# The later modulation sums on TensorE, behind the native tiles, in place of ScalarE and GpSimd

## The reference, cut to what matters

```python
mod = (jax.nn.silu(c) @ w_ada[i] + b_ada[i])[:, None, :]      # w_ada: 2048 x 12288
sh1, sc1, g1, sh2, sc2, g2 = jnp.split(mod, N_MOD, axis=-1)   # six vectors of 2048
hl = rmsnorm(x, norm1_w[i]) * (1.0 + sc1) + sh1
out_l, _, _ = token_mixer(hl, s_f, s_b, grid, lp)             # Hyena and SSD branches
x = x + g1 * out_l
hl2 = rmsnorm(x, norm2_w[i]) * (1.0 + sc2) + sh2
x = x + g2 * sqrelu_mlp(hl2, w_mlp1[i], w_mlp2[i])
```

## Time and profile before

| | |
|---|---|
| median of 3 executions | 4385.58 us (4385.01 to 4386.99) |
| the profiled execution | 4384.95 us |
| its span, first to last instruction | 4383.2 us |
| TensorE busy (matmuls) | 4238.8 us, 97% |
| GpSimd busy | 3536.8 us, 81% |
| VectorE busy | 2403.6 us, 55% |
| ScalarE busy | 1756.3 us, 40% |
| mean granted TensorE clock | 0.981 |

### The profile page before, as it was taken

The page is one execution under the profiler, slowest core; times in us unless marked ns, Lnnn a source line. Parts: engine busy times, 40 slices in busy tenths (PEclk is TensorE's granted clock), DMA queues, the critical chain, the costliest instruction groups (busy, mean ns, idle before and its releaser), DMA issues.

```text
span 4383.2 us, 66380 instructions
## 1 busy us (share of the span) xinstructions
PE 4238.8 (97%) x24638; PEld 3647.1 (83%) x24638; DVE 2403.6 (55%) x3732; ACT 1756.3 (40%) x1994; POOL 3536.8 (81%) x2700
## 2 busy tenths in 40 slices
PE   8999898998999999999999999999999999999998
PEld 6778676587888888888888988899888888888887
DVE  4342466534333335544322432788857957885795
ACT  4333443244444444443344434543334333333433
POOL 5755897077888888888789977987988998898897
PEclk9999898899999999999999999999999999999999
DMA  9834676044555554444455544444554454454453
GB/s 378 332 116 181 251 304 262 0 163 165 182 188 185 186 187 172 164 163 166 159 202 186 208 154 144 176 171 164 183 183 173 174 194 170 172 193 177 174 180 144
DMA packets 116320, 813.72 MB, mean 186 GB/s; under 512 B 13479, under 2 KB 17864, under 8 KB 19016
## 3 DMA queue, kind: packets, MB, share of 16 engines
q1 hardware_dynamic: 109008, 789.40, 49.0%
q10 hardware_dynamic: 7096, 21.20, 1.3%
HBM read 804.26 MB, written 6.29 MB: 185 GB/s over the span
## 4 chain that ended last, share of the span: by engine, by line
PE 62%; POOL 23%; DVE 7%; issue 6%; ACT 1%; DMA 1%; POOLq 0%; SPq 0%; DVEq 0%; ACTq 0%
PE psum L536 30%; POOL w_lo L457 19%; PE psum L540 16%; POOL ada_acc L487 4%; PE psum L525 1%; PE psum L527 1%; PE psum L526 1%; PE psum L688 1%; DVE out_hl L3098 1%; DVE out_hl L3096 1%; PE psum L1286 1%; DVE hid L3094 1%; PE psum L671 1%; PE psum L672 1%; PE psum L673 1%
## 5 line engine op out<-in xcount | busy, mean ns | idle before, releaser
L457 POOL TENSOR_TENSOR w_lo<-ring,w_hi 128x512 fp32r<-128x512 f32 x2416 | 3131.8, 1323 | 600.5 <-ACT w_hi L1362 585.4
L1362 ACT ACTIVATE w_hi<-ring 128x1024 fp32r<-128x1024 f32 x1228 | 1292.2, 1060 | 1856.3 <-PE psum L540 1641.0
L536 PE MATMUL psum<-hc_hl,w_hi 128*128 128x512 f32 x5120 | 1310.8, 398 | 25.6 <-DVE hc_hl L2006 9.7
L536 PEld LDWEIGHTS psum<-hc_hl,w_hi 128*128 128x128 f32 x5120 | 924.3, 189 | 205.5 <-issue 16.9
L540 PEld LDWEIGHTS psum<-hc_hl,w_lo 128*128 128x128 f32 x5120 | 700.2, 191 | 52.6 <-POOL w_lo L457 1.5
L540 PE MATMUL psum<-hc_hl,w_lo 128*128 128x256 f32 x5120 | 715.5, 283 | 1.1 <-POOL w_lo L457 1.1
L536 PE MATMUL psum<-out_hl,w_hi 128*128 128x512 f32 x2048 | 515.2, 393 | 4.4 <-DVE out_hl L3098 2.6
L536 PEld LDWEIGHTS psum<-out_hl,w_hi 128*128 128x128 f32 x2048 | 369.3, 189 | 71.9 <-DVE out_hl L3098 3.4
L487 POOL TENSOR_TENSOR ada_acc<-ada_acc,ada_row 128x512 f32<-128x512 f32 x224 | 288.5, 1318 | 28.6 <-ACT ada_row L1519 21.7
L540 PEld LDWEIGHTS psum<-out_hl,w_lo 128*128 128x128 f32 x2048 | 279.5, 190 | 20.0
L540 PE MATMUL psum<-out_hl,w_lo 128*128 128x256 f32 x2048 | 285.6, 282 | 0.0
(11 more groups left out here) (451 smaller groups left out, 5235.2 us busy)
## 6 DMA issues: line engine op xcount, KB each, us to landing
ring<-stream SPq DMA_DIRECT2D x620, 1024.0 KB, 4.8
ring<-mixed SPq DMA_DIRECT2D x96, 1024.0 KB, 6.4
ada_in<-ada SPq DMA_DIRECT2D x32, 1024.0 KB, 7.4
kv_dram<-kv_out ACTq DMA_DIRECT2D x32, 128.0 KB, 4.1
x<-x ACTq DMA_DIRECT2D x2, 2048.0 KB, 9.7
kv<-kv_dram ACTq DMA_DIRECT2D x2, 2048.0 KB, 9.2
mem_raw<-mem SPq DMA_DIRECT2D x2, 1024.0 KB, 6.4
ctx_raw<-ctx ACTq DMA_DIRECT2D x1, 2048.0 KB, 12.5
```

The lines of the kernel that those rows point to most:

```text
L457: m = pool.tensor_tensor(w_lo[:, slot, c:c + 4], ring[:, s, h * KC // 2 + c:h * KC // 2 + c + 4], w_hi[:, slot, c:c + 4].bitcast(F32), ALU ...
L536: pe.matmul(psum[:, b, :].rearrange("p (s t) -> p s t", s=2), w_hi[:, slot, c], x_hl[c], start=start(c), stop=False, skip_group_check=True)
L1362: act.activation(w_hi[:, 2 * (s % 2) + h], ring[:, s, k], ACT.Copy).then_inc(hi_ready, 1)
```

## The change

The 64 later tiles keep their place in the queue, two behind each native tile, but they are laid out by output columns: pair j holds 256 of the 8192 columns for all 2048 inputs. `ada_row`, `ada_acc`, their semaphores, `scale_rows`, GpSimd's loop, `ada_columns` and `ada_mod` are gone. `native(i)` now ends with `gate_rows(i)`: 16 fp32 matmuls, each with one column of `c_silu` as stationary operand and 256 moving columns, dealt over the four column groups of bank 5. ScalarE copies the bank to a free part of `xbc` (`gate_rows_out`), and behind the next native tile `gate_turn` sums the four groups and turns them into two columns of bank 2. One VectorE addition at the end of the stage adds all biases. SyncE frees the slots of these tiles by `ada_pe`. Bank 5 is new for this, so the heads write banks 4 and 6, the states 4 and 6, and the state products 6 and 4; the second state product and its masks move from head pair 3 to the start.

```diff
@@ SyncE, slot_free
-                sp.wait_ge(ada_scaled, 2 * (m // 3) + m % 3)
+                sp.wait_ge(ada_pe, ADA_1 + 2 * (m // 3) + m % 3)
@@ GpSimd
-        pool.wait_ge(half_done, 2 * FIRST["out1"])
-        for n in range(ADA_2 // KC):
-            for k in range(1, KC):
...
-                for c in range(0, D, 512):
-                    m = pool.tensor_tensor(ada_acc[:, n % 2, c:c + 512],
-                                           (ada_row[:, 0] if k == 1 else ada_acc[:, n % 2])[:, c:c + 512],
-                                           ada_row[:, k % 2, c:c + 512], ALU.add)
-                m.then_inc(ada_done, 2 if k == 1 else 1)
@@ TensorE
             m.then_inc(nat_done, 1)
+            gate_rows(i)
+
+        def gate_turn(j):
+
+            pe.wait_ge(ada_copied, ADA_G + j + 1)
+            for b in range(2):
+                m = pe.matmul(psum[:, 2, 2 * j + b:2 * j + b + 1], xbc[:, 10 + j % 2, 1, b * P:b * P + P],
+                              col("pick", 0), start=True, stop=True)
+            m.then_inc(ada_turned, 1)
+
+        def gate_rows(j):
+
+            if j:
+                gate_turn(j - 1)
+            for half in range(2):
+                m = 3 * j + 1 + half
+                w = ring[:, m % RING].rearrange("p k n -> p (k n)").rearrange("p (k n) -> p k n", n=T)
+                pe.wait_ge(mix_landed[m % RING], 16 * (m // RING + 1 + ADA_1 // 4))
+                for k in range(8):
+                    r = 32 * (k % 4)
+                    i = pe.matmul(psum[r:r + 1, 5, 0:T], c_silu[:, 8 * half + k, 0:1], w[:, k],
+                                  start=half == 0 and k < 4, stop=half == 1 and k >= 4)
+                i.then_inc(ada_pe, 1)
-        def ada_columns(n):
-
-            pe.wait_ge(ada_done, KC * (n + 1))
-            pe.wait_ge(s_mod, n + 1)
-            for k in range(KC):
-                m = pe.matmul(psum[:, 2, k:k + 1], ada_acc[:, n % 2, k * P:k * P + P], const[:, ONES, 0:1],
-                              start=True, stop=True)
-            m.then_inc(ada_sum, 1)
-                m = pe.matmul(psum[:, (2, 6)[n % 2], :], b_nat[:, g, tb], xw[:, tb, :], start=tb == 0, stop=tb == 1)
+                m = pe.matmul(psum[:, (4, 6)[n % 2], :], b_nat[:, g, tb], xw[:, tb, :], start=tb == 0, stop=tb == 1)
-            o = psum[64 * (hh % 2):64 * (hh % 2) + 64, 4 + (hh // 2) % 2, 0:T]
+            o = psum[64 * (hh % 2):64 * (hh % 2) + 64, (4, 6)[(hh // 2) % 2], 0:T]
         state_products(0)
+        state_products(1)
...
-            if p == 3:
-                pe.wait_ge(ssd_cbm, 4)
-                state_products(1)
...
-            if p in (0, 3, 6):
-                ada_columns(p // 3)
-        ada_columns(3)
+        gate_turn(NATIVE - 1)
@@ ScalarE
-                act.activation(ada_row[:, t % 2], w, ACT.Copy, scale=c_silu[:, t % KC, 0:1]).then_inc(ada_scaled, 1)
+        def gate_rows_out(j):
+
+            act.wait_ge(ada_pe, ADA_1 + 2 * j + 2)
+            if j >= 2:
+                act.wait_ge(ada_turned, ADA_G + j - 1)
+            act.activation(xbc[:, 10 + j % 2, 1], psum[:, 5, 0:T], ACT.Copy).then_inc(ada_copied, 1)
@@ VectorE
         state_masks(0)
+        state_masks(1)
...
-        ada_mod(3)
         pair_out(7)
+        dve.wait_ge(ada_turned, ADA_G + NATIVE)
+        dve.tensor_tensor(mod[:, ADA_1:, 0], psum[:, 2, 0:ADA_2], col("b_ada", ADA_1, ADA_2), ALU.add).then_inc(s_mod, 1)
@@ the layout of the weights
-    sums = ada_sums(one["w_ada"][:, ADA_1 * P:]).reshape(NATIVE, 2, P, D)
+    sums = one["w_ada"][:, ADA_1 * P:].reshape(2, 8, P, NATIVE, T).transpose(3, 0, 2, 1, 4).reshape(NATIVE, 2, P, D)
```

More of the change, by code:

```diff
@@ L172, in build @@
     kv_out = at("kv_out", [P, 3, T], 203)
-    ada_acc = at("ada_acc", [P, 2, D], 40)
-    ada_row = at("ada_row", [P, 2, D], 56)
     ctx_raw = at("ctx_raw", [P, KC, T], 176)
@@ L307, in build @@
     nat_done, z_out, hy_out = sem("native_done"), sem("z_out"), sem("hy_out")
-    ada_done, ada_sum, x_full = sem("ada_added"), sem("ada_summed"), sem("x_full")
+    x_full = sem("x_full")
     s_const, s_cols, s_c = sem("const_landed"), sem("columns_landed"), sem("c_landed")
@@ L315, in build @@
     s_csilu, s_mod, s_scales = sem("c_silu_ready"), sem("mod_ready"), sem("scales_ready")
-    ada_scaled = sem("ada_scaled")
     ada_copied, ada_turned = sem("ada_copied"), sem("ada_turned")
@@ L754, in state_products @@
             for tb in range(2):
-                m = pe.matmul(psum[:, 6, tb * T:tb * T + T], xbc[:, 8 + g, 0, tb * P:tb * P + P], xbc[:, 10 + g, 0, :],
+                m = pe.matmul(psum[:, (6, 4)[g], tb * T:tb * T + T], xbc[:, 8 + g, 0, tb * P:tb * P + P], xbc[:, 10 + g, 0, :],
                               start=True, stop=True)
@@ L1535, in _ @@
         for i in range(HEAD_SLOT):
+            if i:
+                gate_rows_out(i - 1)
             if i < ZB:
                 z_gate(i)
-            scale_rows(i)
             if i == 5:
@@ L1544, in _ @@
             slot = HEAD_SLOT + 3 * p
+            gate_rows_out(slot - 1)
             head_exps(2 * p + 1)
-            scale_rows(slot)
+            if slot + 1 < NATIVE:
+                gate_rows_out(slot)
             if p < HEADS // 2 - 1:
@@ L1549, in _ @@
             if slot + 1 < NATIVE:
-                scale_rows(slot + 1)
-                scale_rows(slot + 2)
+                gate_rows_out(slot + 1)
+        gate_rows_out(NATIVE - 1)
         act.wait_ge(hd_y, HEADS)
@@ L1638, in half_high @@
                            flat[:, 2048 + 1024 * q:3072 + 1024 * q], ACT.Copy).then_inc(gn_hi, 1)
-        act.wait_ge(ada_sum, ADA_2 // KC)
         act.wait_ge(y_y, 2)
@@ L1655, in _ @@
         split_stage("out1", RING, KC - RING)
-        act.wait_ge(s_mod, 5)
+        act.wait_ge(s_mod, 2)
         norm_act("x2", x, lambda k: mod[:, 3 * KC + k, 0:1],
@@ L2076, in pair_out @@
             dve.wait_ge(hd_y, 2 * j + 2)
-            dve.scalar_tensor_tensor(y_ssd[:, j], xbc[:, j, 0], col("ssd_d", j), psum[:, 4 + j % 2, 0:T],
+            dve.scalar_tensor_tensor(y_ssd[:, j], xbc[:, j, 0], col("ssd_d", j), psum[:, (4, 6)[j % 2], 0:T],
                                      ALU.mult, ALU.add).then_inc(hd_yc, 1)
@@ L2271, in hy_conv @@
                                      out_[:, :, 0:GRID_W - 1], ALU.mult, ALU.add).then_inc(hy_out, 1)
[L2273 to L2277, removed]
         for n in range(4):
@@ L2289, in _ @@
             dve.wait_ge(ssd_st, 2 * n + 2)
-            dve.tensor_copy(state[:, d, g], psum[:, (2, 6)[n % 2], :]).then_inc(ssd_stc, 1)
+            dve.tensor_copy(state[:, d, g], psum[:, (4, 6)[n % 2], :]).then_inc(ssd_stc, 1)
             if n >= 2:
@@ L2296, in state_masks @@
             c_ = cb[:, g]
-            p6 = psum[:, 6, :]
+            p6 = psum[:, (6, 4)[g], :]
             dve.tensor_copy(c_[:, P:T], p6[:, P:T])
@@ L2337, in _ @@
             slot = HEAD_SLOT + 3 * p - ZB
-            if p == 3:
-                state_masks(1)
             head_decay(2 * p + 1)
@@ L2345, in _ @@
                 pair_out(p - 1)
-            if p in (1, 4, 7):
-                ada_mod(p // 3)
             hy_conv(slot)
@@ L2550, in residual @@
                 add(n // RING - 1, j)
-        dve.wait_ge(s_mod, 5)
+        dve.wait_ge(s_mod, 2)
         st.did(dve.scalar_tensor_tensor(scales[:, 2], mod[:, 4 * KC:5 * KC, 0], 1.0, col("norm2", 0, KC),
@@ L3177, in ada_rows @@
     return tiles.reshape(-1, P, D)
-def ada_sums(w):
-    return w.reshape(KC, P, w.shape[1] // D, D).transpose(2, 0, 1, 3).reshape(-1, P, D)
 def packed_blocks(w, per):
```

6 lines of the change are left out of this document (removed).

## The result

The changed kernel took 4400.02 us (4398.84 to 4400.31, six executions), the kernel before 4385.54 us (4382.44 to 4387.55, six executions). The ratio is 1.0032, with a 95% interval of 1.0022 to 1.0042: the change makes the kernel slower by 14.5 us. The forecast was 4396 us in a range of 4387 to 4414, with 0.65 on slower. The profiled execution has a span of 4397.8 us, 14.6 us more than before.

What follows compares the result with a forecast made beforehand. GpSimd bounds the stage, TensorE close behind; TensorE's summed program ends the last head at 756.9 against 746.2 for no change, so +10.7 us on the median of 4385.58 gives 4396 us, range 4387 to 4414.

Steps and rivals of the forecast that it cites:

- The bound: In the stage, GpSimd bounds with TensorE close behind; TensorE has only 32.9 us idle to take the additions over.
- The sum of the stage: TensorE's program from 385.1: 284.7 us stays, 76.2 added, 6.7 wait, 3.4 half clock, 0.8 copy; last head ends 756.9.
- pair of row matmuls: Added TensorE block per two tiles: 1.94 us, a third of the way from 1.83 to 2.17; 62.1 us in all.
- state matmuls: Work that stays on TensorE: four state matmul pairs of L746 at 1.71 us each, 6.8 us.
- wait before head 0: TensorE's 10.6 us wait before the first head shrinks to 6.7 us, as GpSimd no longer slows VectorE there.
- half clock: TensorE loses 1.7 us behind L735 and once more behind the wait for head 0: 3.4 us together.
- Issue pace: Rival, chance 0.18: row matmuls go at 0.064 us an instruction, 2.17 us a pair, 7.4 us more, 4403 us.
- All waits go: Rival, chance 0.11: pairs of 1.83 us, 3 us wait for head 0, no half clock; 4386 us, nothing won or lost.
- Faster: Rival, chance 0.04: a pair costs what one L608 block costs, 0.97 us; 31 us go, 4365 us.
- The clock: Rival, chance 0.04: one-column row matmuls leave TensorE at half clock, up to 1.7 us a tile; 4420 us if a fourth do.
- The queue: SyncE's ring loads: a native's tile lands in about 8 us, needed 9.4 us after its request; covered by 1 us.
- The end of the stage: After the last head the filter's loads are exposed (four issues, some 2 us landing); L814 starts about 6.4 us later.

Runs made afterwards that it cites:

- the half rows: The changed kernel with 8 of the 16 row matmuls of each pair left out, all loads kept: 4368.13 us, ratio 0.9971 to the kernel before.
- narrow rows: The changed kernel with all 16 row matmuls of a pair, over 128 moving columns instead of 256: 4369.66 us, ratio 0.9973 to the kernel before.
- the change once more: The changed kernel measured again, unaltered, on the same chip as the kernels beside it: 4393.95 us, ratio 1.0035 to the kernel before.

## Why the prediction was right

**The bound.** "TensorE has only 32.9 us of idle time in the stretch that is to take the additions over": right, shown by TensorE's 180.0 busy in 180.0 us and by the half rows, where 27.8 us less of TensorE's work made the kernel 27 us faster.

**The sum of the stage.** From its first native tile to the last head's end the forecast has 756.9 − 385.1 = 371.8 us; the trace has 756.78 − 386.37 = 370.4. The last head ended where the forecast had it, at 756.8 instead of 756.9, and that closeness is luck: the stretch was 1.4 us shorter than forecast, and this execution began it 1.3 us later than the one of before. The start is no effect of the change; in the thirteen traces it lies between 385.0 and 387.0. Term by term:

| term | forecast | measured | over the stage |
|---|---|---|---|
| pair of row matmuls | 1.94 | 1.84 | −3.2 |
| `gate_turn` | 0.44 | 0.43 | −0.3 |
| `rows`, 14 of them behind a row block | 0.99 | 1.09 | +1.4 |
| state matmuls | 1.71 | 1.82 | +0.4 |
| wait before head 0 | 6.7 | 5.57 | −1.1 |
| half clock | 3.4 | 4.4 | +1.0 |

They add up to −1.8 us; the difference was −1.4, and the rest lies in short blocks that the forecast took together. The pair cost what L608's block does, the low end; the third that I added towards the pace of L1286 was not needed. `rows` is 0.10 us dearer directly behind a row block (518.61 to 519.70), in half and narrow rows too, and so is a state. The half clock: 1.7 us in the native tile behind L732, as before, and behind head 0 it reached further than the one tile that I counted: its two matmul groups took 1.76 and 1.84 us where head 1's take 0.91 and 0.96, and the native tile 7.96 instead of 7.01, 2.7 us in all.

**The rivals on the pair's price.** Issue pace (2.17 us a pair) fell by the 1.84 us and by the narrow block. "All waits go" had its pair nearly right, but 5.6 us before head 0 and the half clock stayed. For the issue pace, the 0.12 us that the forecast adds to 32 × 0.064 stands in none of its rows. "Faster" wanted a pair of 0.97 us; the run with half of the matmuls has just that block, and there the kernel is 0.29% faster than before, so that its mechanism is real and only its price did not hold.

**The clock.** The rival in which one-column matmuls leave the clock at half had 0.04 and fell: the granted clock is 1.00 over 180 us in which a block of 2.3 us of them follows every native tile. Its 4420 us was a slip: a fourth of the 54 us is 13.6 us, which makes 4410 us.

**The queue.** "Covered, by 1 us": right in that TensorE waits nowhere for `ring` in the stage. With half of the row matmuls it used three tiles in 8.4 us (573.35 to 581.77) and still waited nowhere, so the cover was about 1 us or more.

**The end of the stage.** This is the term that was mis-sized. I put the start of the group norm's matmuls 6.4 us behind the last head, with "some 2 us to land" for the loads; it was 766.91 − 756.78 = 10.1 us, because `feats` landed 7.1 us after its issue, behind three other small loads and beside the megabyte tiles of `ring`. No row stood behind the 2 us. They are near what the load takes with these tiles held back (at most 1.9 us in that run), so the step that failed is the overlap with the tiles. The sum had a slip besides: 4 × 0.6 + 2 + 1.1 is 5.5 us and not 6.4, which hid 0.9 us of the error.

Of the 3.7 us, 1.3 came back: from L807 to L820 it is 9.4 us, where it was 10.7 before. All of it lies in the 16 matmuls of the norm, which took 5.04 us (766.91 to 771.95, mean granted clock 0.72) instead of 6.34 us (752.65 to 758.99, 0.57), by the busy time by engine of these stretches after and before:

```profile
766.91:771.95 5.04, 5.04 (x18) 3.96 (x17) 2.92 (x8) 1.64 (x2) 0.00 (x0) 0.72 0.88 229
```

```profile
752.65:758.99 6.34, 6.34 (x16) 4.88 (x16) 1.02 (x3) 2.94 (x3) 0.00 (x0) 0.57 0.01 3
```

They ran less of their time at the half clock, which the forecast did not foresee.

So the taps begin 776.32 − 763.37 = 12.95 us later than before. The kernel ended 14.6 us later. The last 1.7 us arise behind it, where the two kernels do the same work. That is less than one kernel differs from itself there: from the second taps on, the profiled execution of the change took 3612.1 us (785.74 to 4397.8), and the one of the change once more 3602.1 us (784.11 to 4386.2), both with the same code. So no cause can be named for it. The forecast of +10.7 us missed the +14.5 by 3.8: 2.4 us net at the end of the stage, the rest behind it. The range held it, the direction was right, and the case that came true was the one forecast.

## What to carry to other kernels

When an engine bounds a stage and the next one is 90% busy beside it, moving all of the work changes the name of the bound: here 72.6 us went to an engine with 33 us free in the stretch. Sum the new bound's own program before moving, and split the work where the two sums meet; half of it beat both kernels, by 0.4% and 0.7%. And ask what was hidden behind the wait that goes: a 33-row load that cost nothing behind the old tail stood 8.5 us in front of the new one.

## What the runs showed of the hardware that was not expected

GpSimd's additions, when they had no pause at all, twice shut VectorE out. In the profiled execution of the run with 240 of them back to back, from the stretch of the second stall (us, PE, PEld, DVE, ACT, POOL, PEclk, DMA, GB/s):

```profile
562.63:626.70 64.07, 0.00 (x0) 0.00 (x0) 64.07 (x3) 0.24 (x1) 63.81 (x64) 0.51 0.00 0
```

GpSimd does 64 additions, VectorE's two instructions of 0.9 us together stand for the whole 64 us, TensorE does nothing. The stall ended with GpSimd's last addition (its unbroken stream ran from 383.41 for 243.03 us, to 626.4); the first one, of 67.9 us, ended at 516.2 in the middle of the stream, and why then is open. Between the two GpSimd added on without pause, and VectorE still ran: its products `xw`, which read SBUF alone, took 2.4 to 3.1 us for two instead of 1.28 us in the kernel after, and its instructions that read PSUM, such as the copy of a state with 0.69 us, were not longer at all. With a pause behind every eight additions `mix_m` took at most 1.30 us instead of 0.48, and nothing stalled. What sets a stall off is not shown: both kinds of run differ in the pauses, but 46 us of the unpaused stream passed without one. A filler of GpSimd work, harmless in its sum, can thus cost some 71 us in the median (1.0194 against 1.0032) and some 124 us in the profiled execution.

Row matmuls with one stationary column in four column groups advance TensorE by 0.031 us an instruction of 128 columns and 0.058 us one of 256 (1.84 / 32): half as many columns, half the time, with no floor seen down to 0.98 us for 32. An instruction of the native tile, on the whole array, costs 0.219 us for the same 256 columns (7.01 / 32), so spreading one-column matmuls over the four groups made each of them 3.8 times cheaper in TensorE's time.
